# Plain activations for the experts, and nineteen places for their weights

## What is computed

```python
h2 = rms_norm_2(x, g_ffn)                       # x * rsqrt(mean(x*x) + eps) * g_ffn
x = x + hier_moe(h2, ...)

def hier_moe(h, wg, bg, we, be, w1, w3, w2):
    pg = softmax(hf @ wg + bg)                  # 4 groups, the best one is taken
    le = (hf @ we + be)...                      # 8 experts of that group, the two best
    gate = pg_sel[:, None] * p_top / sum(p_top)
    ...
    ys = (silu(xb @ w1[e]) * (xb @ w3[e])) @ w2[e]     # per expert, hidden width 512
    out = zeros.at[tok].add(ys * gate)
```

## Time and profile before

| | us |
|---|---|
| median of three runs | 2386.05 |
| the profiled execution, its time | 2386.7 |
| its span | 2385.3 |
| TensorE busy | 2235.4 (94%) |
| VectorE busy | 1365.2 (57%) |
| ScalarE busy | 564.5 (24%) |
| POOL busy | 64.3 (3%) |

### The profile page before, as it was taken

One profiled execution on the slowest core, in us unless ns is written; L12 is line 12 of the kernel. 1 busy time (PEld: TensorE's weight loads), 2 busy tenths in 40 slices (PEclk: granted clock), 3 DMA queues, 4 the chain that ended last, 5 costly groups with the idle time before them and its releaser, 6 DMA issues.

```text
span 2385.3 us, 28950 instructions
## 1 busy us (share of the span) xinstructions
PE 2235.4 (94%) x10686; PEld 1622.8 (68%) x10686; DVE 1365.2 (57%) x3507; ACT 564.5 (24%) x1375; POOL 64.3 (3%) x65
## 2 busy tenths in 40 slices
PE   7988889999999998999999999999799799989887
PEld 6864568888888885558888888888457533333332
DVE  6559757666565667996665665765776311121114
ACT  2013342100011215772100011201583212121110
POOL 0000000000000000000000000000000011111110
PEclk9998799999999999999999999999999799899899
DMA  5220022222233320002223222322004799999997
GB/s 201 88 80 7 17 72 71 89 89 89 89 89 89 111 86 19 1 1 71 88 89 89 86 86 86 97 89 88 1 1 179 281 416 418 417 418 417 417 419 298
DMA packets 69885, 348.11 MB, mean 146 GB/s; under 512 B 10852, under 2 KB 11748, under 8 KB 44208
## 3 DMA queue, kind: packets, MB, share of 16 engines
q1 hardware_dynamic: 64576, 337.13, 38.7%
q0 software_dynamic: 4880, 8.05, 0.9%
q10 hardware_dynamic: 288, 1.05, 0.1%
HBM read 341.00 MB, written 17.30 MB: 150 GB/s over the span
## 4 chain that ended last, share of the span: by engine, by line
PE 75%; DVE 7%; ACT 2%; issue 1%; DMA 1%; DVEq 0%; SPq 0%; ACTq 0%
PE bank L568 25%; PE bank L2518 9%; PE bank L573 7%; PE bank L587 7%; PE bank L580 7%; PE bank L2526 5%; PE bank L559 2%; PE bank L2491 2%; DVE exps L1866 1%; DMA w<-in_experts 1%; DVE square L2661 1%; PE bank L917 1%; PE bank L930 1%; PE bank L942 1%; PE bank L1120 1%
## 5 line engine op out<-in xcount | busy, mean ns | idle before, releaser
L2518 PE MATMUL bank<-w,xT 128*64 128x512 f32 x960 | 215.8, 599 | 4.7 <-DMA w<-in_experts 3.9
L2691 DVE COPY square<-bank 128x256 f32<-128x256 f32 x32 | 13.6, 425 | 353.0 <-ACT rope L2613 353.0
L2518 PEld LDWEIGHTS bank<-w,xT 128*64 128x64 f32 x960 | 68.4, 138 | 145.1 <-issue 135.6
L1343 ACT ACTIVATE exps<-exps,small 128x128 f32<-128x128 f32 (+1 forms) x224 | 124.3, 559 | 100.0 <-DVE small L1866 99.4
L1618 DVE TENSOR_TENSOR third<-first,bank 128x256 f32<-128x256 f32 x106 | 44.7, 421 | 165.1 <-PE bank L568 164.3
L568 PE MATMUL bank<-u,ring 128*128 128x256 f32 x576 | 136.1, 379 | 0.0
L2526 PE MATMUL bank<-w,square 128*64 128x512 f32 x480 | 129.6, 687 | 4.6 <-ACT square L2620 2.9
L568 PE MATMUL bank<-h_sums,w_sum 128*128 128x256 f32 x512 | 121.0, 379 | 0.0
L568 PE MATMUL bank<-h,ring 128*128 128x256 f32 x512 | 120.9, 379 | 0.0
L568 PEld LDWEIGHTS bank<-u,ring 128*128 128x128 f32 x576 | 109.4, 190 | 15.7 <-issue 1.0
L568 PE MATMUL bank<-u_mlp,ring 128*128 128x256 f32 x480 | 113.4, 379 | 0.0
(11 more groups left out here) (456 smaller groups left out, 4233.7 us busy)
## 6 DMA issues: line engine op xcount, KB each, us to landing
w<-in_experts SPq DMA_DIRECT2D x180, 1024.0 KB, 16.9
ring<-in_dense SPq DMA_DIRECT2D x216, 512.0 KB, 4.2
consts<-in_experts SPq DMA_DIRECT2D x12, 1024.0 KB, 19.8
w<-y_pairs SPq DMA_DIRECT2D x4, 1024.0 KB, 26.3
consts<-in_consts SPq DMA_DIRECT2D x1, 2310.5 KB, 16.7
x<-in_xT SPq DMA_DIRECT2D x4, 512.0 KB, 7.1
h_tokens<-u SPq DMA_DIRECT2D x4, 512.0 KB, 3.0
bias_scratch<-y_ab SPq DMA_DIRECT2D x4, 320.0 KB, 2.2
```

Source lines behind the costliest of these rows:

```text
L1343: act.activation(e, e, ACT.Exp, bias=neg[:, a:a + 1], scale=-1.0, accum_out=total[:, a:a + 1]).then_inc(s[done], 1)
L2518: ins = k.pe.matmul(bank[a * CAP:(a + 1) * CAP, :], xT[:, kk % 4, kk // 4, :], w[:, (2 * (kk % 2) + a) * EH:(2 * (kk % 2) + a + 1) * EH], ...
```

## The change

The experts and the router read plain x. The gain is multiplied onto the router's weights (by POOL, once) and onto the gathered, transposed rows (by VectorE, which takes over ScalarE's copy); the tokens' root goes, negated, into the fourth column of the meta table, and from there as a scale per row into the sigmoid's exponential and both VectorE steps on the products up. `um` is no longer made, the token-major copy is plain x and so serves as the array of the output too (`pe_tokens` and `act_tokens` go). There are 19 places for pieces: two in the x buffer, usable once x is transposed, and one from memory that is free, among other things by a smaller scratch of POOL's DMA descriptors. Twelve places (0 to 11) are loaded ahead of the wait for the last dense product, five lie over its buffers, and piece 0 goes out ahead of the wait for the attention output and of the router's weights. `dve_slots` of e+3 is issued ahead of the wait for the products up of e, and ScalarE's copy of `hT` right behind its first exponential. The index chain has four small steps instead of three. The fallback follows suit (left out below).

```diff
--- before.py
+++ after.py
@@ -34,9 +34,10 @@
 CAP = 64
 SETS = 4
 PIECES = 6
-SLOTS = 16
+SLOTS = 19
+EARLY, LATE = 12, 5
 LAST = 3
-LATE = 7
+SCRATCH = 8192
 BUCKETS = 32
 LV = 640
 PIECE = 2048
@@ -1163,7 +1164,7 @@
     act_2_prepare(k)
     act_da(k)
     act_sb(k)
-    act_sum(k, CH_2O, 5, k.um, "g_ffn")
+    act_sum(k, CH_2O, 5, None, None)
 def act_inputs(k, dst, gain, tiles):
@@ -2280,17 +2281,18 @@
 def moe_buffers(k):
     s = k.s
     k.dense.close()
-    s.new("router_in", *(f"w_in{j}" for j in range(SLOTS) if j >= len(W_IN) and not 0 <= j - SLOTS + LATE < RING))
+    s.new("router_in", "router_scaled", *(f"w_in{j}" for j in range(len(W_IN), SLOTS) if not EARLY <= j < EARLY + LATE))
     s.new("routed", "route_shifted", "route_exp")
-    s.new("h_turned", "h_copied0", "h_copied1", "h_stored", "x_turned", "x_copied0", "x_copied1")
+    s.new("h_turned", "h_copied0", "h_copied1", "h_stored")
     s.new("counted_in", "counted", "count_ready")
     s.new("w_used", "slots_ready", "meta_done", "idx_ready", "gathered", "g_turned", "g_copied")
     s.new("sig_exp", "sig_log", "sig_ready", "taken", "both", "hid_done", "hid_turned", "hidT_done", "o_done", *(f"scattered{j}" for j in range(SETS)))
     s.new(*(f"pairs_in{b}" for b in range(NB)), "paired", "last_turned", "last_ready", "last_done", "last_out", "out_added", "out_done")
-    late = list(range(SLOTS - LATE, SLOTS))
-    k.w = {j: k.sb(f"w{j}", [P, PIECE]) for j in late + list(range(SLOTS - LATE - 1))}
+    k.w = {j: k.sb(f"w{j}", [P, PIECE]) for j in [*range(EARLY, EARLY + LATE), *range(2, EARLY)]}
     done = k.cpack.at["swap"][0]
-    k.w[SLOTS - LATE - 1] = k.consts[:, done:done + PIECE]
+    k.w[1] = k.consts[:, done:done + PIECE]
+    for j in range(2):
+        k.w[EARLY + LATE + j] = k.x.rearrange("p k t -> p (k t)")[:, PIECE * j:PIECE * (j + 1)]
     k.meta = k.sums.rearrange("p (b e c) -> p b e c", b=NB, c=4)
     k.pos = k.sb("pos", [P, NB, NE])
     k.S = k.sqp[1].rearrange("p (b t) -> p b t", b=NB)
@@ -2300,7 +2302,7 @@
     k.hT = k.sqp[0][:, 0:2 * P].rearrange("p (c a t) -> p c a t", c=2, a=2)
     k.prod = k.sqp[0][:, 2 * P:4 * P]
     k.oN = [k.sb(f"oN{j}", [P, D // 2]) for j in range(SETS)]
-    k.mt = [k.sb(f"mt{j}", [P, 4]) for j in range(2 * SETS)]
+    k.mt = [k.sb(f"mt{j}", [P, 5]) for j in range(2 * SETS)]
     k.idx = [k.sb(f"idx{j}", [P, 2], I32) for j in range(2 * SETS)]
     k.ST = [k.const(n) for n in ("rope_c", "rope_s", "causal")]
     k.count = k.sb("count", [P, 2], I32)
@@ -2314,6 +2316,7 @@
     k.xtok = k.u.rearrange("p k t -> p (k t)").rearrange("p (b d) -> p b d", b=NB)
     k.htok = [k.xtok[:, b, :] for b in range(NB)]
     k.rtok = k.small[:, 480:496]
+    k.w[0] = k.sb("w0", [P, PIECE])
 def moe(k):
@@ -2351,7 +2354,7 @@
 USED = {p: g + 1 for g, p in enumerate(ORDER)}
-W_IN = ("x_in0", "x_in1", "x_in2", "x_in3", "cmp_k_in", "cmp_v_in", "tables_in")
+W_IN = ("x_in0", "x_in1", "x_in2", "x_in3", "cmp_k_in", "cmp_v_in", "tables_in", "gains_in", "vecs_in", "consts_in")
 def piece(k, e, i):
@@ -2360,8 +2363,8 @@
 def piece_in(k, j):
-    late = j - SLOTS + LATE
-    if 0 <= late < RING:
+    late = j - EARLY
+    if 0 <= late < LATE:
         return k.s[f"ring_in{late}"], 16 * ((N_CH - late + RING - 1) // RING)
     return (k.s[W_IN[j]], 16) if j < len(W_IN) else (k.s[f"w_in{j}"], 0)
@@ -2380,16 +2383,19 @@
 def moe_sync(k):
     sp, s = k.sp, k.s
+    load_piece(k, *ORDER[0])
     sp.wait_ge(s["o_normed"], 8)
     sp.dma_start(k.wr, k.t["router"]).then_inc(s["router_in"], 16)
     for g, (e, i) in enumerate(ORDER):
+        if g == 0:
+            continue
         if g == PAIRS_AT:
             sync_pairs(k)
-        if g == SLOTS - LATE:
+        if g == EARLY:
             sp.wait_ge(s["prod_done"], 7 * N_CH // 2)
-        if g == SLOTS - 3:
+        if g == EARLY + LATE - 1:
             sp.wait_ge(s["combined"], N_CH)
-        if g == SLOTS - 2:
+        if g == EARLY + LATE:
             for b in range(NB):
                 sp.wait_ge(s["h_copied0"], b + 1)
                 sp.wait_ge(s["h_copied1"], b + 1)
@@ -2423,7 +2429,7 @@
             elif b == 1 and h == 1:
                 pe.wait_ge(k.ch7.emptied, k.ch7.n)
             for kk in range(4):
-                ins = pe.transpose(k.bank[4 + 2 * (b % 2) + h][:, kk * P:(kk + 1) * P], k.um[:, 4 * h + kk, b * P:(b + 1) * P], k.const("ident"))
+                ins = pe.transpose(k.bank[4 + 2 * (b % 2) + h][:, kk * P:(kk + 1) * P], k.x[:, 4 * h + kk, b * P:(b + 1) * P], k.const("ident"))
             ins.then_inc(s["h_turned"], 1)
     n_b = NB * NE
     before = k.hN[:, 0:n_b + NE]
@@ -2438,8 +2444,6 @@
     pe_x_turn(k, 0)
     for e in range(NE + 1):
         pe_expert(k, e)
-        if 0 <= e - X_TURN < NB:
-            pe_tokens(k, e - X_TURN)
     pe_last(k, NE - 1)
@@ -2447,38 +2451,25 @@
     pe, s, ch = k.pe, k.s, k.ch7
-    pe.wait_ge(s["router_in"], 16)
+    pe.wait_ge(s["router_scaled"], 1)
     for kk in range(KT):
         if kk == 0:
             pe.wait_ge(s["combined"], 2 * (N_CH // 2 - 1))
-            pe.wait_ge(s["u_ready"], 46)
         if kk == KT - 2:
             pe.wait_ge(s["sums_ready"], 7 * 6)
             pe.wait_ge(ch.emptied, ch.n)
             for b in range(NB):
                 ins = pe.matmul(ch.bank[:, 4 * b:4 * b + 4], k.sums[:, b * P:(b + 1) * P], k.const("ones")[:, 0:4], start=True, stop=True)
             ch.end(ins, "norm_ffn")
-            pe.wait_ge(s["u_ready"], 48)
+            pe.wait_ge(s["combined"], N_CH)
         for b in range(NB):
-            ins = pe.matmul(k.bank[b][:, 0:NG + NE], k.um[:, kk, b * P:(b + 1) * P], k.wr[:, kk, :], start=kk == 0, stop=kk == KT - 1)
+            ins = pe.matmul(k.bank[b][:, 0:NG + NE], k.x[:, kk, b * P:(b + 1) * P], k.wr[:, kk, :], start=kk == 0, stop=kk == KT - 1)
     ins.then_inc(s["routed"], 1)
-AHEAD, X_TURN = 3, 4
-TOKEN_BANKS = (3, 6)
-
-
-def pe_tokens(k, b):
-
-    pe, s = k.pe, k.s
-    for h in range(2):
-        if b:
-            pe.wait_ge(s[f"x_copied{h}"], b)
-        for kk in range(4):
-            ins = pe.transpose(k.bank[TOKEN_BANKS[h]][:, kk * P:(kk + 1) * P], k.x[:, 4 * h + kk, b * P:(b + 1) * P], k.const("ident"))
-        ins.then_inc(s["x_turned"], 1)
+AHEAD = 3
 def pe_meta(k, e):
@@ -2490,10 +2481,7 @@
     for b in range(NB):
         ins = pe.matmul(k.bank[7][:, 0:4], k.S[:, b, :], k.meta[:, b, e, :], start=b == 0, stop=b == NB - 1)
     if e >= NE - LAST:
-        if e == NE - LAST:
-            pe.wait_ge(s["x_copied0"], NB)
-            pe.wait_ge(s["x_copied1"], NB)
-        else:
+        if e > NE - LAST:
             pe.wait_ge(s["last_ready"], e - NE + LAST)
         for b in range(NB):
             turned = pe.transpose(k.bank[6][:, b * P:(b + 1) * P], k.S[:, b, :], k.const("ident"))
@@ -2589,7 +2577,6 @@
     act, s = k.act, k.s
     act_root(k, "norm_ffn", k.ch7, k.ch7.bank[:, 0:4 * NB], k.rtok, D)
     act.wait_ge(s["prod_done"], 7 * N_CH // 2)
-    act.wait_ge(s["root_ready"], k.root_at["norm_ffn"])
     for b in range(NB):
         if b == 1:
             act.wait_ge(s["route_shifted"], 1)
@@ -2598,48 +2585,42 @@
             act.activation(k.eight[1], k.eight[1], ACT.Exp).then_inc(s["route_exp"], 1)
         for h in range(2):
             act.wait_ge(s["h_turned"], 2 * b + h + 1)
-            act.activation(k.htok[b][:, h * T:(h + 1) * T], k.bank[4 + 2 * (b % 2) + h], ACT.Copy,
-                           scale=k.rtok[:, 4 * b:4 * b + 1]).then_inc(s[f"h_copied{h}"], 1)
-    act.wait_ge(s["h_stored"], 16 * NB)
+            act.copy(k.htok[b][:, h * T:(h + 1) * T], k.bank[4 + 2 * (b % 2) + h]).then_inc(s[f"h_copied{h}"], 1)
     half = EH // 2
     sig = k.sig[:, 0:half]
     for e in range(NE + 1):
-        if e == 0:
-            act_gathered(k, 0)
         if e < NE:
             act.wait_ge(s["w_used"], up_used(e))
+            act.wait_ge(s["idx_ready"], e + 1)
             if e:
                 act.wait_ge(s["hid_done"], e)
-            act.activation(sig, k.bank[2][:, 0:half], ACT.Exp, scale=-1.0).then_inc(s["sig_exp"], 1)
+            act.activation(sig, k.bank[2][:, 0:half], ACT.Exp, scale=minus_root(k, e)).then_inc(s["sig_exp"], 1)
+        if e:
+            act.wait_ge(s["hid_turned"], e)
+            act.copy(k.hT.rearrange("p c a t -> p (c a t)"), k.bank[4][:, 0:2 * P]).then_inc(s["hidT_done"], 1)
+        if e < NE:
             act.wait_ge(s["sig_exp"], e + 1)
             act.activation(sig, sig, ACT.Ln, bias=1.0).then_inc(s["sig_log"], 1)
             act.wait_ge(s["sig_log"], e + 1)
             act.activation(sig, sig, ACT.Exp, scale=-1.0).then_inc(s["sig_ready"], 1)
         if e:
-            act.wait_ge(s["hid_turned"], e)
-            act.copy(k.hT.rearrange("p c a t -> p (c a t)"), k.bank[4][:, 0:2 * P]).then_inc(s["hidT_done"], 1)
-        if e + 1 < NE:
-            act_gathered(k, e + 1)
-        if e:
             act_out(k, e - 1)
-        if 0 <= e - X_TURN < NB:
-            act_tokens(k, e - X_TURN)
-
-
```

(45 more changed lines are left out.)

26 lines of the change are left out of this document (13 added, 13 removed).

## The result

The changed kernel took 2372.36 us (median of five runs, 2370.92 to 2376.46) beside 2385.88 us of the kernel before (median of five), a ratio of 0.9949 (95% interval 0.9934 to 0.9963). That is 13.5 us less; forecast were 7.9 us less and a range of 2374 to 2383. The direction was right, the time lies 1.6 us under the range. A second set, beside the experiments, gave 0.9960 (0.9944 to 0.9976), 9.5 us less. The two intervals overlap between 0.9944 and 0.9963.

The account below looks back on a forecast made before the run. The prediction took the stream of expert weights, about 15.7 us per expert, as the bound. Its terms −7.5 + 0.3 − 0.7 gave −7.9 us, a median of 2378.2 us, with a range of 2374 to 2383.

Parts of the forecast that it names:

- The bound: Expert stage: the end is set by weight pieces coming through a full stream at 417 GB/s, not by TensorE's work.
- Nineteen places, minus 7.5: Head of the weight stream: three more pieces issued early fill 7.5 of 11.6 idle us, minus 7.5 us.
- Piece 0 first, router weights, scratch, plain x: nothing: Earlier piece 0, later router weights, smaller POOL descriptor scratch and norm on rows: each taken as 0 us.
- Start of expert 0, plus 0.3: Longer index chain starts expert 0's products up 0.7 us later; the hole behind expert 0 gives back 0.4; plus 0.3 us.
- Tail, minus 0.7: Behind the last products up: the copy of hT comes two ScalarE steps earlier, minus 0.7 us, between 0 and 0.8.
- In a stream of 15.7 us per expert this buys nothing.: Expert stage: TensorE's cycle falls from 13.78 to 12.3 us, but it only waits for weights sooner; no gain.
- The allowance for chance: Range of the time: 2 us on either side of the forecast's bounds, since the three runs lie 4.4 us apart.
- The falling clock: Rival, expert stage: TensorE's waits for weights lower its clock to 1.2 GHz; about 2391 us, 5%.
- The places bring less: Rival, weight stream: only one or two of the three places count; gain 1 to 5 us, 2381 to 2385, 15%.
- More: Rival: hole near 1900 closes whole and tail at full clock, or slots free sooner; 10 to 12 us gain, 8%.

Follow-up runs that it names:

- e3: Changed kernel with 16 places again instead of 19 (9 ahead of the last dense product): median 2381.11 us, ratio to before 0.9987.
- e2: Kernel before with only the smaller DMA descriptor scratch (8192): median 2385.53 us, ratio 0.9998.
- e6: Kernel before with one edit, slots of e+3 compared ahead of the wait for the products up of e: median 2382.75 us, ratio 0.9986.
- e8: Changed kernel with ScalarE's copy of hT behind its third function again: last products down wait 1.60 us, last product up to end 32.2 us.
- e4: Changed kernel with the slots compared late again, behind the second product on the hidden: median 2387.94 us, ratio to before 1.0014.
- e1: Kernel before, unchanged, run again for a second trace: 2382.30 us.
- e16: Kernel before, unchanged, run for a third trace: 2385.57 us.
- e13: Changed kernel with the slots compared late, same kernel as e4, for a second trace: 2390.51 us.
- e15: Changed kernel with the slots compared late, same kernel as e4, for a fourth trace: 2395.23 us.
- e5: Changed kernel, nothing altered, run again: median 2375.27 us, ratio to before 0.9960.
- e12: Changed kernel with expert 0's gathered rows transposed earlier and 4, 3 and 1 unread matmuls added in TensorE's idle time: 2372.79 us, ratio to before 0.9950.

## Why the prediction was right or wrong, point by point

- **The bound.** Right: the stream at 417 to 418 GB/s, its pauses for want of places, the end following the landings (rows of the chain above).
- **Nineteen places, minus 7.5.** Right in the changed kernel: 7.2 by e3 against its first trace, 7.8 against the mean of its two. But the term stood on TensorE waiting long enough to use them, and I read 15.7 us for that where its matmuls waited 5.5. By that estimate it is the faster cycle, put at nothing below, that makes room for the whole 7.5; the places alone were not run.
- **Piece 0 first, router weights, scratch, plain x: nothing.** The list shows piece 0 ahead of nothing, and e2 shows the scratch at nothing. The rest was not tried by itself.
- **Start of expert 0, plus 0.3.** The later start was of the right size: from SyncE's first issue to expert 0's products up it is 72.3 and 71.5 us in the changed kernel, and 71.0, 71.9 and 71.0 in the three traces of before, 0.6 more in the mean (0.7 forecast). What the hole behind expert 0 gives back was put too low, 0.4 for the 1.6 of e6: expert 1 starts 84.7 and 83.0 us behind the first issue, in the mean no later than the 83.8 of before.
- **Tail, minus 0.7.** 1.1 by the time from the last product up to the end (31.0 for 32.1), 0.9 by e8's wait: over the bound of 0.8.
- **"In a stream of 15.7 us per expert this buys nothing."** This step failed. The cycle was sized well (12.3 forecast, 12.05 measured), as were the wait of 1.5 us and the end of it. But the step compared 13.78 us with 15.7 and took the 1.9 us between for slack. TensorE's mean cycle with lapses was (2311.08 − 1884.03) / 29 = 14.7 us, and it was left with 5.5 us of waits for weights in the whole stage. The runs show what the move is worth: alone in the kernel before 3.3 us (0.7 to 5.7, e6), with the rest of the change but 16 places much the same (3.1, e3), and taken back in the changed kernel 13 to 15.6 (e4), where TensorE never waits for a weight. I had the lapses in a row of my own, and used it only for the fear that starving would bring more. It went the other way. In all eight traces with TensorE's wait in the middle of each expert the clock lapsed between 1900 and 2340 us (before, e1, e2, e16, e4, e13 to e15); in the ten without it, never (after, e3, e5 to e12). Of e6's 3.3 us its trace shows 1.6 at the head of the stream; that the rest comes from runs in which TensorE with its lapses falls behind the stream is likely by e13 and e15, and not shown, for no trace of the kernel before caught one.
- **The allowance for chance.** The second failure, in the line "so the range takes 2 us on either side". The stretch ahead of the stage, the same work in every kernel, took 1804.7 to 1813.5 us in 18 traces, and the same comparison of kernels gave 13.5 us in one set and 9.5 in the other. By the traces the stage fell by 8.4 us in the mean, or by 8.9 from SyncE's first issue, where the sum had 7.9. Of the first pair's 13.5 us, 6.3 lie ahead of the stage and are chance. The second set's median, 2375.27, is inside the range of 2374 to 2383; with the step above wrong, that would have been luck.
- **The rivals.** The falling clock did not come in the changed kernel. Lapses came in e4, at a smaller price than the one I gave (an expert at the low level taking twice as long): experts with a lapse took 15.9 to 17.6 us there in mid-stage, the others 14.2 or 14.3. "The places bring less" fell with e3. "More" was nearest; of its reasons the hole behind expert 0 shows in e6, and the lapses it did not name.

What stays open: how the 1 to 5 us between the stage's 8.4 and the 9.5 to 13.5 of the two sets divide between chance and long runs of the kernel before. None of its runs above 2387 us left a trace. That its upper runs (up to 2391.9) are of e13's kind is likely by e6 and e3, and not shown.

The Trainium skill (TensorE: Matmul & The Clock Gate, "HAM oscillation — how this bites in real kernels") let me give the clock a rival of its own. It tells of a kernel whose waits for data were some 3 to 5 us each. Here no matmul waited longer than 2.7 us for weights, between groups of eight matmuls, and the clock was 1.00 over 440 us: the rival did not come, but that section is not contradicted either, since no matmul here waited that long for weights.

## What to carry to other kernels

Where two engines run within some 10% of each other, the one that isn't the bound in a trace can be the bound in other runs, or once the first bound is relieved: compare its mean cycle, lapses and all, with the other's, not its best one. A short wait that sat between transposes and small products in every expert cost more than its length here, since TensorE's clock fell with it; the cure was cheap, to issue another engine's work one wait earlier. Before waits are added up, see whether the view counts the weight loads beside the matmuls. And split a difference of two spans at the last point that the change can't have touched, before the sum is judged by it.

## What the runs showed of the hardware that I had not expected

- Starving didn't lower the clock here, and a smaller regular wait did: 60.6 us of waits for weights at 1.00, against 43.4 us of waits for slots at 0.95. What TensorE did around the latter: six transposes (1 us), 1.5 us of waiting, eight products of four columns (1.05 us). With the same transposes and products and no wait between them (e6) the clock was 1.00.
- Fourteen full matmuls that nobody reads, put where the changed kernel's TensorE waits five times (8.9 us in all) between the router and expert 0, kept the clock at 1.00 and took 2.9 us off the next 32 products.
